# First attention layer: score maps in pairs, with padded keys and biases added by TensorE, and index scores and top-k placed among the projections

## The reference

```python
aq, ackv, akr, aqi, aki, awi, bq, bk, bv, bf = split_cols(u @ w_in, AB_WIDTHS)   # 512,256,16,512,64,8,512,512,512,8
# dsa: index scores choose 64 keys for each query
rel = relu(einsum('bqhd,bsd->bqhs', qi, k_idx))
score = where(causal, einsum('bqhs,bqh->bqs', rel, wi), -inf)
_, idx = top_k(score, 64)
logits = (qa . c_sel + qr . kr_sel) * scale;  p = masked_softmax(logits, valid);  o_a = p . c_sel . w_uv
# fox: causal attention with a forget term
cum = cumsum(log_sigmoid(bf + b_forget))
logits = bq . bk * scale + cum[query] - cum[key];  o_b = masked_softmax(logits, causal) . bv
h = h + concat(o_a, o_b) @ w_out
```

## Time and profile before

| | |
|---|---|
| median of 3 runs | 1042.9 us (1037.14 to 1049.56) |
| the profiled execution | 1028.74 us, its span 1026.9 us |
| mean granted clock of TensorE in it | 0.961 of full speed |
| busy: PE, DVE, ACT, POOL | 974.5, 637.3, 500.8, 262.2 us |
| chain that ended last: PE, DVE, ACT | 89%, 5%, 3% |

### The profile page before, as it was taken

How to read it: one execution, slowest core, us unless ns; L and a number is a source line. 1 busy time by engine, 2 the same in 40 slices (tenths; PEclk the granted TensorE clock), 3 DMA queues, 4 the chain that set the end, 5 groups by cost and what they waited for, 6 DMA issues and landing times.

```text
span 1026.9 us, 16405 instructions
## 1 busy us (share of the span) xinstructions
PE 974.5 (95%) x5426; PEld 819.9 (80%) x5426; DVE 637.3 (62%) x1114; ACT 500.8 (49%) x977; POOL 262.2 (26%) x300
## 2 busy tenths in 40 slices
PE   9998998999999989999899999999899999999946
PEld 7886677899999978777779999998787887878734
DVE  5565645555555569555455555555657788778853
ACT  6454234544444455445344444444646556555532
POOL 0110120222222220134302222222151533714530
PEclk9998989999999999999899999999899999999957
DMA  9553003455555537500045555555364554544401
GB/s 364 185 169 99 1 0 104 140 188 185 184 186 186 188 127 240 159 1 2 21 144 166 188 190 184 191 186 184 120 195 136 164 164 143 168 159 161 145 1 41
DMA packets 40509, 147.83 MB, mean 144 GB/s; under 512 B 4496, under 2 KB 4752, under 8 KB 40464
## 3 DMA queue, kind: packets, MB, share of 16 engines
q1 hardware_dynamic: 40176, 147.07, 43.3%
q10 hardware_dynamic: 288, 0.17, 0.1%
HBM read 146.18 MB, written 1.05 MB: 143 GB/s over the span
## 4 chain that ended last, share of the span: by engine, by line
PE 89%; DVE 5%; ACT 3%; issue 2%; DMA 1%; POOL 1%; DVEq 0%; SPq 0%; POOLq 0%; ACTq 0%
PE acc L310 17%; PE acc L312 17%; PE acc L311 17%; PE misc L383 3%; PE misc L310 3%; PE misc L311 3%; PE ptp L310 3%; PE misc L312 3%; PE ptp L311 3%; PE ptp L312 3%; PE pair L363 3%; PE pair L654 2%; DVE wl L397 1%; PE acc L900 1%; PE pair L356 1%
## 5 line engine op out<-in xcount | busy, mean ns | idle before, releaser
L397 DVE TENSOR_TENSOR wl<-raw,wh 128x1024 fp32r<-128x1024 f32 x273 | 339.9, 1247 | 250.6 <-ACT wh L392 250.1
L392 ACT ACTIVATE wh<-raw 128x1024 fp32r<-128x1024 f32 x273 | 288.0, 1058 | 290.4 <-PE acc L312 171.1
L310 PE MATMUL acc<-wh,xh 128*128 128x512 f32 (+3 forms) x552 | 221.9, 402 | 2.7 <-issue 1.5
L312 PE MATMUL acc<-wh,xl 128*128 128x512 f32 (+3 forms) x552 | 215.0, 389 | 0.0
L311 PE MATMUL acc<-wl,xh 128*128 128x512 f32 (+3 forms) x552 | 214.7, 389 | 0.0
L1401 POOL TENSOR_TENSOR hq<-hr 128x256 f32<-128x256 f32 x64 | 85.9, 1342 | 259.8 <-ACT hr L1127 259.8
L310 PEld LDWEIGHTS acc<-wh,xh 128*128 128x128 f32 x552 | 105.4, 191 | 26.5 <-issue 6.0
L312 PEld LDWEIGHTS acc<-wh,xl 128*128 128x128 f32 x552 | 105.0, 190 | 21.8
L311 PEld LDWEIGHTS acc<-wl,xh 128*128 128x128 f32 x552 | 105.5, 191 | 18.7
L310 PE MATMUL acc<-wh,hh 128*128 128x512 f32 x256 | 100.0, 391 | 1.0 <-DVE hl L1624 1.0
L312 PE MATMUL acc<-wh,hl 128*128 128x512 f32 x256 | 100.8, 394 | 0.0
(11 more groups left out here) (291 smaller groups left out, 1510.6 us busy)
## 6 DMA issues: line engine op xcount, KB each, us to landing
raw<-stream SPq DMA_DIRECT2D x273, 512.0 KB, 3.3
h<-x SPq DMA_DIRECT2D x2, 512.0 KB, 4.3
out<-h SPq DMA_DIRECT2D x2, 512.0 KB, 3.1
cst<-consts SPq DMA_DIRECT2D x1, 1018.0 KB, 10.6
row<-rows SPq DMA_DIRECT2D x1, 764.0 KB, 12.0
col<-cols ACTq DMA_DIRECT2D x1, 106.0 KB, 5.2
cst<-consts ACTq DMA_DIRECT2D x1, 64.0 KB, 4.0
```

What stands on the lines that cost most here:

```text
L310: nc.tensor.matmul(out_, ah, bh, start=start, stop=False, skip_group_check=True)
L312: return nc.tensor.matmul(out_, al, bh, start=False, stop=stop_, skip_group_check=True)
L392: nc.scalar.activation(wh[:, u % SPLIT, :], raw[:, u % RAW, :], ACT.Copy).then_inc(w_hi, 1)
L397: nc.vector.tensor_tensor(wl[:, u % SPLIT, :], raw[:, u % RAW, :], wh[:, u % SPLIT, :].bitcast(F32), ALU.subtract).then_inc(w_lo, 1)
```

## The change

Layer 0 gets the pipeline of layer C. The functions of that pipeline are made common (`scores`, `turn_p`, `mix` on PE; `exponentials`, `p_first` on ACT; `peaks`, `p_second`, `scaled` on DVE), with steps numbered through both layers. Layer 0 then has 8 steps of two heads each: four for fox, four for dsa. Keys are written to SBUF twice, multiplied by a 0/1 column (`C_HALF`). The forget term is added by a float32r product of a selector with `decay`, a tile that holds high and low parts of the sums; the causal mask by the identity, as in layer C; and for dsa a chosen-keys mask `picked` by the identity. The selectors come by a transfer of their own (512 KB, which leave the table `consts`) and are copied by POOL.

The order of the projections changes: latent and small pieces first (352 columns), then index queries, queries of dsa, the two expansions, and queries, keys and values of fox. All eleven pairs of transposes, the four index-score products (two heads each), four of eight top-8 passes and the first two steps' scores stand between units. The rope of the dsa queries moves from DVE to POOL. The matmuls of zeros in `maps` are gone; 12 and 6 at the kernel's start remain.

```diff
-AB_ORDER = (6, 7, 1, 2, 4, 5, 9, 3, 0, 8)
...
+AB_ORDER = (1, 2, 4, 5, 9, 3, 0, 6, 7, 8)
...
+        AB_Z = ((pair[0], head_pairs(AQI)), (pair[1], head_pairs(AQI + 2 * P)),
+                (ptp, [[kid[:, t, a, :] for t in range(T)] for a in range(2)]),
+                (pair[0], head_pairs(AQ)), (pair[1], head_pairs(AQ + 2 * P)),
+                (ptp, ka_pairs(0)), (misc, ka_pairs(2)),
+                (pair[0], head_pairs(BQ)), (pair[1], head_pairs(BQ + 2 * P)),
+                (ptp, head_pairs(BK)), (misc, head_pairs(BK + 2 * P)))
+        NZ_AB = len(AB_Z)
...
+            nc.sync.dma_start(sel_stage, sel_d).then_inc(sel_in, 16)
...
-            def maps(ms, fill, extra=None, between=None):
...
+            def scores(st, q, keys, bias):
+                if st >= 2:
+                    pe.wait_ge(s_exped, 2 * (st - 1))
+                banks = [c_bank(st, t).rearrange("p (a k) -> p a k", a=2) for t in range(T)]
+                for t in range(T):
+                    mm(banks[t], q[:, t * P:(t + 1) * P], keys[:, :, 0:(t + 1) * P],
+                       start=True, stop=False, skip_group_check=True)
+                for t in range(T):
+                    bias(banks[t], t).then_inc(s_scored, 1)
...
+            def turn_p(st, a):
+                pe.wait_ge(s_exped, 2 * st + a + 1)
+                pe.wait_ge(s_copied, 2 * st + a)
+                pb = probs[:, st % 2, :]
+                for k, c0 in enumerate((a * P, 2 * P + a * SEQ, 3 * P + a * SEQ)):
+                    last = nc.tensor.transpose(ptp[:, k * P:(k + 1) * P], pb[:, c0:c0 + P], ident)
+                last.then_inc(s_turned, 1)
+            def mix(st, v):
+                pe.wait_ge(s_copied, 2 * st + 2)
+                if st >= 1:
+                    pe.wait_ge(s_scaled, st)
+                for a in range(2):
+                    last = pe_pv(misc[:, a * P:(a + 1) * P], c_pt(st, a), v(a), HD)
+                last.then_inc(s_mixed, 1)
...
+            def ab_scores(st):
+                if st < FOX:
+                    def bias(bank, t):
+                        n = (t + 1) * P
+                        for a in range(2):
+                            mm(bank[:, a, :], selr[:, 2 * st + a, :], decay[:, 0:n], start=False, stop=False,
+                               skip_group_check=True)
+                        return causal(bank, t)
+                    scores(st, QK[:, B_QB + st, :], fox_keys(2 * st, 2), bias)
+                else:
+                    def bias(bank, t):
+                        k0, n = TK[t][1:]
+                        return mm(bank, idr[:, :], picked[:, k0:k0 + n].unsqueeze(1).broadcast_to([P, 2, n]),
+                                  start=False, stop=True, skip_group_check=True)
+                    i = st - FOX
+                    if i == 0:
+                        pe.wait_ge(picked_set, 1)
+                    scores(st, QK[:, B_QA + i, :], QK[:, B_KA + 2 * i:B_KA + 2 * i + 2, :], bias)
...
+            def ab_iter(it):
+                if 0 <= it - 2 < STEPS_AB:
+                    turn_p(it - 2, 0)
+                if it < STEPS_AB:
+                    ab_scores(it)
+                if 0 <= it - 2 < STEPS_AB:
+                    turn_p(it - 2, 1)
+                if 0 <= it - 3 < STEPS_AB:
+                    if it == 3:
+                        pe.wait_ge(ev_act, left(G_ABO))
+                        pe.wait_ge(ev_dve, left(G_ABO))
+                    mix(it - 3, ab_values(it - 3))
...
+                if u == U_KV + 1:
+                    pe.wait_ge(z_act, 2)
+                    pe.wait_ge(z_dve, 1)
+                    pe.wait_ge(dve_prep, 4)
+                    idx_scores(0)
+                if u == U_QB:
+                    idx_scores(1)
+                if u in (U_QB + 1, U_QB + 2):
+                    y = u - U_QB + 1
+                    pe.wait_ge(idx_relu, y - 1)
+                    idx_scores(y)
+                if u == U_KB:
+                    pe.wait_ge(q_roped, 2)
+                    pe.wait_ge(idx_relu, 4)
+                    ab_turn(3)
+                    ab_turn(4)
+                if u == U_KB + 2:
+                    pe.wait_ge(ev_act, left(G_QB))
+                    pe.wait_ge(ev_dve, left(G_QB))
+                    ab_turn(5)
+                    ab_turn(6)
+                if u == U_KB + 3:
+                    pe.wait_ge(ev_act, left(G_KB))
+                    pe.wait_ge(ev_dve, left(G_KB))
+                    pe.wait_ge(z_act, 3)
+                    pe.wait_ge(z_dve, 2)
+                    ab_turn(7)
+                    ab_turn(8)
+                if u == U_VB:
+                    pe.wait_ge(ev_act, left(G_VB))
+                    pe.wait_ge(ev_dve, left(G_VB))
+                    pe.wait_ge(pad_act, 2)
+                    pe.wait_ge(pad_dve, 2)
+                    ab_turn(9)
+                    ab_turn(10)
+                if u == U_VB + 2:
+                    pe.wait_ge(masks_set, 2)
+                    pe.wait_ge(sel_set, 1)
+                    pe.wait_ge(decay_set, 1)
+                    pe.wait_ge(z_act, 4)
+                    pe.wait_ge(z_dve, 3)
+                    pe.wait_ge(pad_act, 4)
+                    pe.wait_ge(pad_dve, 4)
+                    ab_iter(0)
+                if u == U_VB + 3:
+                    ab_iter(1)
...
+            for g, u0, w in ((G_AB, U_AB, AQI), (G_QI, U_QI, GW), (G_QA, U_QA, GW)):
+                pe_group(pe, g, u0, 4, w, block_b=0 if g == 0 else None, after=lambda uu, u0=u0: between(u0 + uu))
             pe.wait_ge(c_lo, 1)
             pe_group(pe, G_KV, U_KV, 1, A_HEADS * NOPE, k0=KD)
-            pe_group(pe, G_KV + 1, U_KV + 1, 1, 512, k0=KD)
-            def ab_ready(j):
-                if j == 8:
-                    pe.wait_ge(dve_prep, 3)
-                    pe.wait_ge(ev_act, left(G_KV + 2))
...
-            for y in range(IDX_HEADS):
...
-            maps(AB_MAPS, FILL_AB, forget)
-            pe.wait_ge(o_out, 16)
+            pe_group(pe, G_KV + 1, U_KV + 1, 1, 512, k0=KD, after=lambda uu: between(U_KV + 1))
+            for g, u0 in ((G_QB, U_QB), (G_KB, U_KB), (G_VB, U_VB)):
+                pe_group(pe, g, u0, 4, GW, after=lambda uu, u0=u0: between(u0 + uu))
+            for it in range(2, STEPS_AB + 3):
+                ab_iter(it)
+            pe.wait_ge(s_scaled, STEPS_AB)
             pe_turn_block(pe, 1, o_tok)
...
+                         view=lambda v: v.rearrange("p (h e) -> p h e", h=A_HEADS))
+                if u == U_QB:
+                    evac(act, G_KV + 1, U_QB, 0, va[:, 0, :], rr(S_CKV), 512)
+                if U_QB <= u < U_QB + 4:
+                    relu(u - U_QB)
...
+                    even_keys(9, fox_keys(0, 4)[:, 0::2, :])
+                    act.wait_ge(pad_dve, 3)
+                    even_keys(10, fox_keys(4, 4)[:, 0::2, :])
+            for it in range(1, STEPS_AB + 2):
+                if 0 <= it - 2 < STEPS_AB:
+                    p_first(it - 2)
+                if it - 1 < STEPS_AB:
+                    exponentials(it - 1)
+                if it == 1:
+                    evac(act, G_VB, U_ABO, 0, Y[:, 0, BV:BV + GW], rr(N_A0), GW)
+            act.sem_inc(z_act, 2)
...
+            g.memset(kid[:, :, :, :], 0.0)
+            g.memset(decay[:].bitcast(F32), 0.0)
...
+            g.tensor_copy(selr[:, :, :].rearrange("p h q -> p (h q)"), sel_stage).then_inc(sel_set, 1)
...
+            def coefficients(st):
+                pool.wait_ge(s_exped, 2 * st + 2)
+                return g.tensor_tensor(c_stat(rs, st), c_stat(su, st),
+                                       mone[:, 0:1].unsqueeze(2).broadcast_to([P, 2, T]), ALU.pow)
+            for it in range(STEPS_AB):
+                coefficients(it).then_inc(s_coef, 1)
...
+            def idx_sums(y):
...
+            TOP_AT = (U_KB + 1, U_KB + 2, U_VB + 2, U_VB + 3)
+            for u in range(U_ABO):
+                split(u + LEAD)
+                if u == U_QI:
...
+                    evac(dve, G_KV + 1, U_QB, 1, va[:, 1, :], rr(S_CKV), 512)
+                if U_QB < u <= U_QB + 4:
+                    idx_sums(u - U_QB - 1)
+                if u == U_KB:
+                    evac(dve, G_QB, U_KB, 1, Y[:, 1, BQ:BQ + GW], rr(N_A0), GW)
+                if u == U_KB + 1:
+                    turned_out(4, QK[:, B_QA + 2:B_QA + 4, :], SCALE)
+                if u in TOP_AT:
                     top8()
-                if m == N_KEEP // 8 - 1:
...
+            for it in range(STEPS_AB + 3):
+                if it < STEPS_AB:
+                    peaks(it)
+                if 0 <= it - 2 < STEPS_AB:
+                    p_second(it - 2)
+                st = it - 3
+                if st >= 0:
+                    c0 = 2 * HD * st + 512 if st < FOX else 2 * HD * (st - FOX)
+                    scaled(st, o_tok[:, :, c0:c0 + 2 * HD].rearrange("p t (a d) -> p a t d", a=2), rs)
+                if it == 0:
+                    evac(dve, G_VB, U_ABO, 1, Y[:, 1, BV:BV + GW], rr(N_A0), GW)
```

(27 more changed lines are left out.)

639 lines of the change are left out of this document (283 added, 356 removed).

## The result

The change made the kernel faster: a median of 1001.4 us (997.5 to 1002.3, 4 runs) against 1040.9 us (1037.1 to 1049.6, 4 runs), 39.6 us less. The ratio is 0.960, with a 95% interval of 0.953 to 0.967. The prediction was right in sign and in the stages, and too small in size: it said 25 us, 1018, in a range from 1005 to 1033, and 1001.4 lies outside it.

The account below looks back on a forecast made before the run. TensorE bounds it: full in layer 0's projections, then busy through a 76.2 us stretch with 23.1 us of zeros. Turning 29.1 us earlier less 4.0 of clock gives 25: 1042.9 - 25 = 1018 us, range 1005 to 1033.

Parts of the forecast that it names:

- The projections: Layer 0's projection units: work put between them adds 8.0 us of TensorE time; the last unit ends at 91.8, helpers covered.
- Rival A: Helpers DVE, ACT, POOL fall behind in the projections: 1028 us, chance 0.17; shown if the last value unit ends past 96.
- The DVE chain and the wait: Behind the projections: DVE back to back to T + 12.1 with four top-8 passes; TensorE idle about 6.6 us.
- T: The end of the last value unit of layer 0's projections, forecast at 91.8 us.
- Iterations and end: Layer 0's new pipeline: 3.7 us for each of iterations 4 to 7, then layer C's end, 8.35 us.
- The clock behind the wait: TensorE's first two or three us of work after the 6.6 us wait run at half speed, costing 2 us.
- The low stretch at the end: End of layer 0's pipeline: chance one half of a low clock like layer C's end, 4 us, counted as 2.
- The turning of the outputs: End of layer 0's pipeline: starts at T + 39.1 = 130.9 instead of 160.04, 29.1 us earlier, before clock costs.
- The runs' median, 1042.9, lies 14.2 above that; I carry the difference: Last step, whole kernel: 14.2 us between profiled execution and runs' median added to 1003.7, giving 1018 us.
- the old stretch had two, already in the 76.2: Stretch behind the old projections: its two low clock stretches, mean 0.91, were already counted in its 76.2 us.
- rival B: Pipeline behind the projections: wait under 3 us, clock stays up, end as layer C's; gain 29 to 33, 1012; chance 0.12.
- the reason for a low pipeline: Layer 0's new pipeline: six transposes a step, not counted as busy, and no zeros would keep the clock low; no gain.

## Why the prediction was right, and where it failed

**The projections: right.** Forecast: the last unit ends 8.0 us later, at 91.8. Measured 92.9, 1.1 more. The helpers covered their part: TensorE is busy 81.22 of 81.90. Rival A did not happen; its sign, 96 or later, is 3 us off.

**The DVE chain and the wait: right, the wait somewhat smaller.** Forecast: ops back to back from T + 1 to T + 12.1 with four passes, TensorE idle 6.6 us. Measured: back to back until 102.72, which is T + 9.8, and idle 5.23. TensorE stopped at 97.63, T + 4.7 for T + 5.5, and DVE was ahead by more: it was done with the last low part and the pass behind it at 92.06, 0.8 before T and not 1.0 after it, and each op cost about what it was priced at (maxima 1.02, passes 1.3 to 1.4). Leaving the passes out took 4.2 of the 5.2 us away: they were its price in the main, as said.

**Iterations and end: right.** 3.60 measured for 3.7, and 8.28 (123.37 to 131.65) for 8.35.

**The clock behind the wait: right in kind.** One low stretch, 6.8 us long, between 100 and 108, of which the wait covers the first part; it cost 2.0 us (iteration 3 above), the 2 forecast. The low stretch at the end, to which the prediction gave a chance of one half (2), is missing in this trace and stands in the second trace of the changed kernel. The turning of the outputs was forecast at 130.9 before clock costs and came at 131.65 with them.

**The step that failed is the last one: "The runs' median, 1042.9, lies 14.2 above that; I carry the difference".** It treats the 14.2 us as something that both kernels have. The changed kernel does not have it: its median lies 3.9 us above its profiled execution (1001.4 and 997.5). It was low clock, and in the one further trace that there is of the kernel before it lies inside the stretch that the change removes: "the old stretch had two, already in the 76.2" was not true of it, for the same stretch is 98.5 us there, at 0.69. So 14.2 - 3.9 = 10.3 of the 16.6 us by which 1018 missed come from this step, and without them the forecast would have been 1007.7. The hint stood in the numbers ahead: the profiled execution lay 8 us below the fastest of the three runs shown, so it differed from them in something.

The other 6.2 us are the distance between the two traces, 31.2 where the sum said 25. The outputs are turned 1.3 us earlier than forecast with the 2 of clock behind the wait (131.65 for 132.9), and the other 4.8 are clock behind the turning: 2 were set aside for a low stretch that this trace does not have, and there the kernel before has one more, 2.8. Both are low stretches that come and go from one execution to the next. The traces thus differ by what rival B gave, 29 to 33, but not in B's way: the wait is 5.2 us, not under 3, and the clock did fall. And that the sum without its last step, 1003.7, comes close to 1001.4 is luck: it is a figure for the profiled execution, which took 997.5.

What the 39.6 us are can be estimated by span times clock. It falls from 986.9 to 962.8 between the two traces, so some 24 us are work and waits that are gone, and the other 16 are clock, of which the medians show more than the two traces do. The zeros alone are some 21 of such us (medians of 984 and 964 with and without them on one chip): the change saves little more than the zeros, and what it adds is that the clock stays up without them. The experiments split it in another order. Full rows alone are worth 1044.7 - 1018.4 = 26 us by the medians, all clock; from there to the changed kernel are 1018.4 - 1001.4 = 17, some 22 less by span times clock, with a part given back in low clock at the wait. The two come from different chips, so they need not add up to 39.6.

The Trainium skill (TensorE: Matmul & The Clock Gate, Part 1) puts the clock down to how busy TensorE has been. The trace of the kernel before again disagrees, with TensorE busy 58.00 of 58.00 us at 0.54. For gaps the trace of the changed kernel agrees: in and behind the wait of 5.23 us the clock was low.

The Trainium skill (TensorE: Matmul & The Clock Gate, Part 4) says that transposes don't count as the other matmuls do, and the prediction weighed this as the reason for a low pipeline. With six transposes to an iteration the pipeline ran 22.67 us at 1.00, and the same six with half the rows in the scores ran at 0.51 over 58 us: here the score products decided.

**What stays open.** Why an execution of the kernel before now and then keeps its clock (1019.9 and 1020.2 us, both at 0.969) and mostly not: no run shows what differs between two executions of it. And what exactly adds up to a high clock: the 8-row product, half rows and missing zeros pull it down in company, no one of them was shown to do it alone, and rows are not separated from the numbers in them.

## What to carry to other kernels

Compare the profiled execution with the runs before the sum: where it is faster than all of them, look at its mean clock, and if the change removes the stage in which the clock varies, do not carry the difference. Multiply span and mean clock of every run: where the product is the same and the times are not, the clock is the difference. Running a product over 128 rows in place of 64 costs nothing in columns and, in this kernel, went with a clock of 1.00 where it was half; full rows without zeros (1023.4) also beat zeros with half rows (1037.1, the same chip), of which the zeros took 23 us and held the clock only sometimes. Work put behind the last large stage on the engine that feeds it should be moved one stage earlier if the cover allows: two top-8 passes of 1.4 us moved so, and the other two one step later, were worth 7 us; spreading all four without moving any was worth 2.

## What was not expected of the hardware

- TensorE busy without a gap, 58.00 of 58.00 us, ran at a granted clock of 0.54. Its work was f32 scores over 64 rows, 8-row products and zeros, with transposes and products with values between.
- The same kernel took 1019.9 to 1059.1 us on one chip, with mean clocks of 0.969 to 0.929. The changed kernel, on two chips, stayed within 5 us.
- Scores over 64 rows in place of 128, with all other instructions alike, took the new pipeline from 1.00 to 0.51 and an iteration from 3.60 to 7.53 us.
- Seventy matmuls on zeros over 128 rows did not keep the clock, and without them it fell in all of ten runs (0.924 to 0.935).
- Span times mean clock was 981.6 to 988.5 us in 44 executions of the kernel before, whose times went from 1019.9 to 1059.1.
